# Expert retrieval with gathers of 4 slots x 32 tokens, summed in four column groups of TensorE

## The reference

```
q = (xb @ w_query).reshape(128, 8 heads, 2, 128)
s = einsum("thse,sne->thsn", q, sub_keys)          # 128 keys in each half
s1, i1 = top_k(s[:, :, 0], 16);  s2, i2 = top_k(s[:, :, 1], 16)
cand = s1[..., :, None] + s2[..., None, :]         # 16 x 16 sums
cidx = i1[..., :, None] * 128 + i2[..., None, :]
top, pos = top_k(cand, 16);  idx = take_along_axis(cidx, pos)
gate = softmax(top)
hid = einsum("thkd,td->thk", expert_u[idx], xb)
act = gelu(hid) * gate
out = einsum("thk,thkd->td", act, expert_v[idx])
```

## Time and profile before

| | |
|---|---|
| median of 3 runs | 2213.87 us (2211.97 to 2216.14) |
| the profiled execution: its time, its span | 2209.7 us, 2207.9 us |
| busy in the span: PE, DVE, ACT, POOL | 84%, 67%, 19%, 43% |
| loads by the gathers | 671.13 MB in 640 gathers |
| mean granted clock of TensorE | 0.956 of full speed |

### The profile page before, as it was taken

One profiled execution on the slowest core, in us unless ns is written; L12 is line 12 of the kernel. 1 busy time (PEld: TensorE's weight loads), 2 busy tenths in 40 slices (PEclk: granted clock), 3 DMA queues, 4 the chain that ended last, 5 costly groups with the idle time before them and its releaser, 6 DMA issues.

```text
span 2207.9 us, 20751 instructions
## 1 busy us (share of the span) xinstructions
PE 1845.6 (84%) x5920; PEld 923.3 (42%) x5920; DVE 1486.1 (67%) x3712; ACT 422.2 (19%) x1223; POOL 942.3 (43%) x1088
## 2 busy tenths in 40 slices
PE   4897999996888888888788888788888888888886
PEld 2473557553334334334334334344333344334332
DVE  7821112314787877887877887877877877887874
ACT  3320110403211111221111221211211111211211
POOL 6316650001454444444454444454444454444451
PEclk8998996997999999999999999999999999999999
DMA  6208530602999999999999999999999999999995
GB/s 223 99 1 152 162 114 1 277 0 102 417 416 418 413 408 419 407 389 421 410 411 418 393 397 421 415 409 417 406 368 422 414 414 416 389 401 422 417 417 235
DMA packets 132023, 731.49 MB, mean 331 GB/s; under 512 B 11776, under 2 KB 46336, under 8 KB 48208
## 3 DMA queue, kind: packets, MB, share of 16 engines
q0 software_dynamic: 92160, 671.13, 74.3%
q1 hardware_dynamic: 35536, 57.06, 7.6%
q10 hardware_dynamic: 4224, 2.10, 1.0%
HBM read 727.10 MB, written 3.15 MB: 331 GB/s over the span
## 4 chain that ended last, share of the span: by engine, by line
PE 56%; DVE 22%; issue 15%; DMA 4%; ACT 2%; DVEq 0%; SPq 0%; POOL 0%; ACTq 0%; POOLq 0%
PE bank L598 29%; PE bank L578 6%; PE bank L474 4%; DVE mix_r L1173 3%; PE bank L547 2%; PE bank L370 2%; DMA r<-w_mod 2%; DMA r<-table,gidx 2%; PE bank L431 2%; DVE r L1167 2%; PE bank L514 1%; DVE mix_r L1141 1%; DVE mix_r L1147 1%; DVE i L1115 1%; DVE mix_r L1146 1%
## 5 line engine op out<-in xcount | busy, mean ns | idle before, releaser
L598 PE MATMUL bank<-r,mix_r 128*128 128x512 f32 x2560 | 1217.9, 616 | 282.9 <-DVE mix_r L1173 282.1
L1283 POOL DMA_INDIRECT r<-table,gidx x640 | 772.0, 1206 | 1081.1 <-PE bank L598 632.1
L1167 DVE CUSTOM_DVE_ANT_0 r<-r,mix_r 128x1024 f32<-128x1024 f32 x640 | 781.8, 1222 | 205.0 <-DMA r<-table,gidx 187.8
L598 PEld LDWEIGHTS bank<-r,mix_r 128*128 128x128 f32 x2560 | 467.4, 193 | 941.5 <-DVE mix_r L1173 520.0
L845 ACT ACTIVATE mix_r<-mix_r 128x1 f32<-128x1 f32 x640 | 128.4, 201 | 1020.5 <-DVE mix_r L1167 1020.0
L1173 DVE TENSOR_SCALAR mix_r<-ident,mix_r 128x128 f32<-128x128 f32 x640 | 225.3, 352 | 65.5 <-ACT mix_r L845 64.3
L578 PE MATMUL bank<-r,hT_r 128*128 128x256 f32 x640 | 147.0, 383 | 3.5 <-ACT hT_r L726 3.5
L578 PEld LDWEIGHTS bank<-r,hT_r 128*128 128x128 f32 x640 | 123.1, 193 | 36.9 <-issue 21.8
L474 PE MATMUL bank<-hT_r,r 128*128 128x512 f32 x192 | 85.6, 599 | 1.3 <-DVE mix_r L1031 1.3
L370 PE MATMUL bank<-r,cond 128*2 128x256 f32 x384 | 50.7, 424 | 42.8 <-DMA r<-w_mod 39.8
L1114 DVE MAX8 mix_r<-mix_r 128x8 f32<-128x128 f32 x80 | 19.5, 285 | 64.3 <-ACT mix_r L837 64.3
(11 more groups left out here) (239 smaller groups left out, 1510.2 us busy)
## 6 DMA issues: line engine op xcount, KB each, us to landing
r<-w_mod SPq DMA_DIRECT2D x24, 1024.0 KB, 7.6
r<-table,gidx POOLq DMA_INDIRECT x640, 10.1
r<-w_query SPq DMA_DIRECT2D x8, 1024.0 KB, 15.2
r<-w_tiles SPq DMA_DIRECT2D x14, 512.0 KB, 3.5
r<-w_o SPq DMA_DIRECT2D x2, 2048.0 KB, 9.6
hT_r<-xT SPq DMA_DIRECT2D x1, 2560.0 KB, 15.6
x_r<-xT SPq DMA_DIRECT2D x1, 2560.0 KB, 17.4
y_out<-r SPq DMA_DIRECT2D x5, 512.0 KB, 23.9
```

The lines of the kernel that those rows point to most:

```text
L598: last = mm(bank[ACC[G // HEADS % 2][h]][:, :], diag[:, k % 4, :], rows[:, k % SLOTS, D + h * 512:D + (h + 1) * 512], start=False, stop=Fa ...
L1167: V.tensor_tensor_reduce(rows[:, s, 0:D], rows[:, s, 0:D], h2c[G // HEADS % 2], 1.0, 0.0, ALU.mult, ALU.add, hid[:, par, k:k + 1]).then_in ...
L1283: G_.indirect_dma_start(rows[:, k % SLOTS, :], None, table, bass.IndirectOffsetOnAxis(gidx[:, e, k:k + 1], 0)).then_inc(row_in[k % SLOTS], 16)
```

## The change

**Shape of a gather.** A gather now holds 4 slots of 32 tokens: partition 32 s + m of gather k = 4 g + tg holds token 32 tg + m and its slot 4 g + s. There are still 16 gathers in a head, of 128 rows each, into the same 8 buffers, and gather n still waits for the sum of gather n - 8.

**Weights and sums.** gelu runs on four columns at a time. `weigh` (VectorE) makes four weights of 128x32 at once: gelu x gate times `fold`, a constant of four 32x32 identities one above the other. It stands behind dot 4 g + 5, that is, two dots into the next four. `add_rows` adds four gathers: for each half of 512 columns one matmul for each 32 tokens, into partitions 32 tg to 32 tg + 31 of the bank, so into four column groups of TensorE. `v_done` rises with each of the last four.

**Hidden vectors.** Since the four token groups stand in the same partitions, there are four token-major copies, `h2r[tg]`, each with 32 tokens repeated four times. `turn_hidden` makes one after the other by 32 matmuls in PSUM banks 4 and 5, and TensorE waits for ScalarE's copy of one before it writes the next. A copy for the next block can only be taken once the last dot of this block that reads the old one is done.

**Experts and gates.** They are computed token by token, and must reach the new layout: `spread_experts` (TensorE, 16 small matmuls with slices of the identity), then `take_experts` on VectorE (before dot 12), which raises `topk_done`.

**Also.** `query` is computed transposed (16 matmuls of 128 columns for 8 of 256), which does away with `query_turn` and one copy; `clear` goes, since the first sum of a block starts the bank; small copies on VectorE go.

```diff
+TG = 32
+NTG = P // TG
-        h2c = [mx(0, 1024), mx(1024, 1024)]
+        h2r = [mx(0, 1024), mx(1024, 1024), mx(2048, 1024), r1[:, 16384:17408]]
...
-            def add_rows(G, k):
-
-                pe.wait_ge(diag_ready, G * TOPK + k + 1)
+            def spread_experts(t):
+
+                pe.wait_ge(gi_ready, t + 1)
+                for s in range(4):
+                    for tg in range(NTG):
+                        last = mm(bank[3][TG * s:TG * s + TG, 8 * tg:8 * tg + 8], ident[:, TG * tg:TG * tg + TG], gi[:, :, 4 * s:4 * s + 4],
+                                  start=True, stop=True)
+                last.then_inc(gi_mm, 1)
+
+            def add_rows(G, g):
+
+                pe.wait_ge(wgt_ready, 4 * G + g + 1)
                 for h in range(2):
-                    last = mm(bank[ACC[G // HEADS % 2][h]][:, :], diag[:, k % 4, :], rows[:, k % SLOTS, D + h * 512:D + (h + 1) * 512],
-                              start=False, stop=False, skip_group_check=True)
-                last.then_inc(v_done, 1)
+                    for tg in range(NTG):
+                        s = (4 * g + tg) % SLOTS
+                        last = mm(bank[ACC[G // HEADS % 2][h]][TG * tg:TG * tg + TG, :], wgt[:, g % 2, tg, :],
+                                  rows[:, s, D + h * 512:D + (h + 1) * 512],
+                                  start=(G % HEADS == 0 and g == 0), stop=(G % HEADS == HEADS - 1 and g == 3))
+                        if h:
+                            last.then_inc(v_done, 1)
...
+                for tg in range(NTG):
+                    pe.wait_ge(h2c_ready, NTG * b + tg)
+                    for k in range(KD):
+                        t0 = b * P + tg * TG
+                        for s in range(4):
+                            last = mm(bank[4 + k // 4][TG * s:TG * s + TG, (k % 4) * P:(k % 4 + 1) * P], hT[:, k, t0:t0 + TG], ident[:, :],
+                                      start=True, stop=True)
+                    last.then_inc(h2c_mm, 1)
...
             query(0)
-            query_turn(0)
             scores(0)
+            pe.wait_ge(h_ready, 3 * KD)
             turn_hidden(0)
-            clear(0)
-            for G in range(NBLK * HEADS):
+            spread_experts(0)
+            for G in range(NALL):
...
+                if t < NALL:
+                    query(t)
+                    scores(t)
+                for g in range(4):
+                    if g == 0 and head == 0 and b >= 2:
+                        pe.wait_ge(peer_ev, b - 1)
+                    if g == 3 and head == HEADS - 1 and b < NBLK - 1:
+                        turn_hidden(b + 1)
+                    if g == 2 and t < NALL:
+                        spread_experts(t)
+                    add_rows(G, g)
...
-            def gelu(G, par, k):
-                act.wait_ge(dot_done, G * TOPK + (k + 1))
+            def gelu(G, par, g):
+                act.wait_ge(dot_done, G * TOPK + 4 * g + 4)
...
+            def take_hidden(b, tg):
+
+                act.wait_ge(h2c_mm, NTG * b + tg + 1)
+                if b:
+                    act.wait_ge(dot_done, (b * HEADS - 1) * TOPK + 12 + tg + 1)
...
-            def make_diag(G, par, k):
-                dve.wait_ge(gelu_done, G * TOPK + (k + 1))
-                dve.wait_ge(v_done, G * TOPK + (k + SLOTS - 3))
-                ts(diag[:, k % 4, :], ident[:, :], gel[:, par, k:k + 1], gate[:, par, k:k + 1], ALU.mult, ALU.mult).then_inc(diag_ready, 1)
+            def weigh(G, par, g):
+
+                n = 4 * G + g
+                wl = Chain(dve, act_done, n)
+                dve.wait_ge(gelu_done, n + 1)
+                a = gel[:, par, 4 * g:4 * g + 4]
+                wl(tt(a, a, gate[:, par, 4 * g:4 * g + 4], ALU.mult))
+                if n >= 2:
+                    dve.wait_ge(v_done, 4 * (n - 1) + SLOTS)
+                tt(wgt[:, g % 2, :, :], fold[:, :].rearrange("p (a m) -> p a m", a=1).broadcast_to([P, NTG, TG]),
+                   a.rearrange("p (g m) -> p g m", m=1).broadcast_to([P, NTG, TG]), ALU.mult).then_inc(wgt_ready, 1)
...
                     dot(G, e, k)
-                    if k:
-                        make_diag(G, e, k - 1)
+                    if k % 4 == 1 and G * 4 + k // 4:
+                        weigh(*((G, e, k // 4 - 1) if k > 4 else (G - 1, 1 - e, 3)))
```

More of the change, by code:

```diff
@@ L574, in query, with scores @@
                     pe.wait_ge(sc_ev, t)
[L575 to L579 removed]
+                for h in range(2):
+                    for k in range(KD):
+                        if t == 0 and h == 0:
+                            pe.wait_ge(h_ready, KD + k + 1)
+                        last = mm(bank[2][:, h * P:(h + 1) * P], wq[:, k, col0 + h * P:col0 + (h + 1) * P], hT[:, k, blk * P:(blk + 1) * P],
+                                  start=(k == 0), stop=(k == KD - 1))
                 last.then_inc(q_mm, 1)
[L582 removed]
+            def scores(t):
                 pe.wait_ge(q_ev, t + 1)
[L584 to L589 removed]
                 for h in range(2):
@@ L1102, in _ @@
                 tt(hT[:, k, CTX:T], xt[:, k, CTX:T], rs2[:, CTX:T], ALU.mult).then_inc(xs_ready, 1)
-            for b in range(NBLK):
-                last = V.tensor_copy(g2b[:, b, :], modT[:, 5 * KD:6 * KD, min(b, 1)])
-            link(last)
-            NT = 26
+            NT = 25
             def best_keys(cl, t):
@@ L1196, in _ @@
             cl = Chain(dve, topk_seq)
-            for n in range(6):
+            for n in range(5):
                 topk_stage(cl, 0, 0, n)
+            experts_and_gates(cl, 0, 0)
+            take_experts(cl, 0, 0)
             assert cl.n == NT, cl.n
-            for G in range(NBLK * HEADS):
+            for G in range(NALL):
                 b, head = G // HEADS, G % HEADS
```

205 lines of the change are left out of this document (88 added, 117 removed).

## The result

| | before | after |
|---|---|---|
| median, four runs each on one chip | 2215.01 us (2211.97 to 2219.1) | 3056.12 us (3047.82 to 3064.03) |
| span of the profiled execution | 2207.9 us | 3046.0 us |
| mean granted clock | 0.956 | 0.669 |

The ratio is 1.3795, with a 95% interval from 1.3751 to 1.3839. The time lies in the predicted range (2870 to 3620), 244 us under the point of 3300, and close to the 3080 of the rival with four column groups at once.

What follows compares the result with a forecast made beforehand. DMA engines bound the kernel before; batching would empty the gather queue every four gathers. 157 periods of 16.4 us lead to 2616, plus 60 and 40: loop 2716 for 1649; with +17 and +3, 3297, stated as 3300 us; range 2870 to 3620.

Steps and rivals of the forecast that it cites:

- the rival with four column groups at once: TensorE's sums: all four groups run side by side, first `v_done` after 1.72 us plus low clock; 3080 us, chance 20%.
- steps 1 to 7: From one group's first gather start to the next: second landing, dot, `weigh`, TensorE start, sums, gather start, low clock; 16.4 us.
- the ring: Way round the buffers: gathers wait for sums, sums for weights, weights for landings; predicted 16.4 us for four gathers.
- The rival that the queue does not run empty: Gather queue: DMA engines stay full, way round a group under 10.0 us; total near 2170 us, chance 4%.
- Step 5: TensorE's sums: two records at a time, the tenth through after six steps of 0.43 us; 2.58 us to the first `v_done`.
- steps 5 to 7: TensorE's sums 2.58 us, end of the sum to the gather's start 1.04, loss to the low clock 1.95.
- T4: Period of four gathers in the loop, from one group's first start to the next: 16.4 us, ends 13.7 and 17.8.
- 1, start to second landing: Gathers into an empty queue: from a group's start to its second landing 9.0 us, ends 8.46 and 9.56.
- 2, dot: VectorE's dot after the second landing, up to the next instruction: 1.15 us.
- 3, `weigh`: VectorE's two products that make the weights: 0.65 us for both, between 0.4 and 0.8.
- top 16, whole loop: VectorE's top 16 stages, late because `query` queues behind sums: 1.5 us in each of 39 heads, 60 us, lower end 0.
- block ends, whole loop: Last sums of a block wait for the hidden-vector copies: 8 to 10 us four times, 40 us, at least 0.

Runs made afterwards that it cites:

- the dose: The changed kernel with `weigh` behind the first, second (the change itself) or third dot of the next four gathers: 2589.27, 3056.12 and 3395.5 us.
- the two half changes: Kernel before, four diagonals made together, `query`, `query_turn`, `scores` ahead of the head's first sum: 3212.99 us; changed kernel with gelu, weights, sums per gather: 2216.77 us.
- the exchanged loops: The changed kernel with the two loops of the sums swapped, both halves of one column group before the next group: 3024.11 us.
- the two filled kernels: The changed kernel plus unread matmuls: fourteen behind each group's sums, 3338.53 us; or eight behind `scores` and twelve behind most other sums, 2944.65 us.

## Why the prediction was right, and where it was off

**The mechanism was right, one term was not.** The steps 1 to 7 are the ring that the timeline shows, the shares of DMA and GB/s, the trains of four dots and the clock came as described, and the dose (6.59, 9.40, 11.53 us to the dot, then 6.08) and the two half changes (1.4518 for the batch, 1.0018 for the rest alone) leave no other cause for the bulk of the 840 us. The low clock is a part of the way round, by some 270 us as estimated above. The rival that the queue does not run empty fails at the point named: the way round would have to be under 10 us, and is 15.4.

**Step 5 was read wrongly**, and the rival "all four column groups at once" was right. From the earlier trace rows I concluded that two records run at a time *whatever the number of groups*. The rows have only two groups, so they could not tell "two at a time" from "as many as there are groups". The first `v_done` comes after four steps of 0.853 us, 3.41, and the gather 1.0 later, so 4.40 from TensorE's start; steps 5 to 7 had 2.58 + 1.04 + 1.95 = 5.57. The rival's 1.72 + 1.72 + 1.04 = 4.48 is it nearly. (With it its terms add up to a T4 of 15.3 us, not the 15.2 stated, and so to some 3095 us for 3080.) For the rule of the Trainium skill, page TensorE: Matmul & The Clock Gate (Part 3), the runs show one half: the near full side by side of column tiles holds here (four at a time); that matmuls start in program order does not hold for the exchanged loops.

**The other terms.** Each against its measured size:

| step | predicted | measured |
|---|---|---|
| 1, start to second landing | 9.0 us | 9.40 |
| 2, dot | 1.15 | 1.15 |
| 3, `weigh` | 0.65 | 0.48 |
| 5 to 7, sums to the gather | 5.57 | 4.40 |
| period T4 | 16.4 | 15.43 |
| top 16, whole loop | 60 | not seen |
| block ends, whole loop | 40 | 17 |
| start | +17 | +11 against the last squares |
| end | +3 | +0.5 |

Over 157 periods the 0.97 us make 152 of the 244 us. The top 16 was to delay 1.5 us in each head; the medians of the four periods of a head are 15.2, 15.5, 15.8 and 15.3 us, none longer by such an amount. The sums take 2 to 3 us less than in step 5's reading and leave TensorE to `query` earlier, which is more than the 1.5 us; I take that for the reason, and no run tried it apart. The block ends: four periods of 19.1, 19.2, 19.3 and 20.9 us, 17 us together beyond 15.43. I had counted the matmuls of the copies in two groups, as in step 5, at 3.4 us for a copy. They too run in four: 16 records of 128 columns in one group took as long in the kernel before (its `clear`) as the 64 of one copy do now, when the clock is high.

```profile
525.29 1.95 PE L616 MATMUL bank<-zeros 128*128 128x128 f32 x16
```

```profile
531.72 1.95 PE L619 MATMUL bank<-ident,hT_r 128*32 128x128 f32 x64 [1.21 <-ACT mix_r L851]
```

In the profiled execution the first gather came only 3.2 us later than before, since its mixers ended 8 us earlier.

For the second landing, 9.40 lies between the two ends that I kept; and the shortest time to landing is 5.3 us (the profile of the change has no landing for the first gather of a group; with `weigh` behind the third dot, where it has, they take 5.57 us in the median and 5.26 at least). For it the formula of the Trainium skill, page DMA: Bandwidth & Descriptors (Anatomy of one DMA), gave an estimate of 4.4, and no run here comes as low.

**Clock.** Step 7 had 1.95 us. The four steps at 0.853 for 0.43 are 1.7 us, and a group at the high clock is 1.73 us faster to its gather; so the term was nearly right, and the 0.84 and 1.08 us of the two filled kernels are what they gave back with part of their groups at the high clock.

That the time lies in the range owes something to luck: the case it was centred on, two records at a time, did not come, and the range held because it was drawn to take in most of the first rival.

## What to carry to other kernels

Before work is batched, write down the way round a buffer: start, landing, what is computed, release. Batching by four adds the landings that the first of the batch now waits for, and where this brings the way round over (buffers x time of a transfer) the bound engine runs dry in every turn, however much cheaper each step has become. The place of the releasing instruction in an engine's order is worth more than its cost: here one dot, 2.5 us, moved the kernel by 340 to 470 us, and 5 to 6% stay even at the best place that was tried.

And a trace that has two of something can't tell what four would do: such a reading deserves even chances, not 62 to 20.

## What the runs showed of the hardware

- Matmuls that write to four different column groups start four at a time (0.853 us a step of 512 columns at the low clock, 0.43 at the high), and they do so when the program has all the matmuls of one group ahead of those of the next (four starts within 0.06 us).
- Extra matmuls raised the granted clock from 0.669 to 0.896 and made the kernel faster by 111 us where nothing waited behind them, but slower by 161 and 282 us where `query` did (2506.37 for 2345.68, where the exponentials were moved too, and 3338.53 for 3056.12). From TensorE's start to the gather took 2.66 us at the high clock and 4.39 at the low.
- The same 640 gathers took more time of the DMA engines when issued in fours: the queue's share of the span is 71.3% of 2350.9 us, 1676 us, with `weigh` behind its own last dot, and 74.3% of 2207.9, 1640 us, in the kernel before; in the change, whose queue runs empty in each period, it is 57.8% of 3046.0, 1761 us. A part of this lies right behind a start in an empty queue: 57 GB/s at a share of 0.32 and 229 at 0.84 in two windows of 1 us, for 426 at 1.02 later. Why is open.
